# Normalizing attention weights inside the product that turns them, by a diagonal of reciprocal sums

## What is computed

```
# even layer of the first stack ("diff"): 4 heads, 2 components of width 64, values of width 128, causal, blocks of 128 queries
p = softmax(q k^T)                       # (component, query, key)
w = p[0] - lam * p[1]
out = w @ v
# odd layer ("odd"): 3 dilated patterns, 4 heads of width 128; a query sees up to 512 + 128 + 128 keys, one softmax over all of them
# second stack, even layer ("rope"): 8 query heads on 2 key heads of width 64, 256 context + 512 latent keys
sc = q k^T * scale;  pr = softmax(sc);  out = pr @ v
```

## Time and profile before

| | |
|---|---|
| median of 3 executions | 3251.61 us (3250.78 to 3253.14) |
| profiled execution: its time, its span | 3251.17 us, 3249.4 us |
| mean granted TensorE clock | 0.996 of full |
| TensorE busy (matmul, weight load) | 3195.2 us (98%), 2817.9 us (87%) |
| VectorE, ScalarE, GpSimd busy | 2307.3 us (71%), 1490.6 us (46%), 513.2 us (16%) |
| "diff", first score to the next slab | 182.87 to 230.28 us |
| "odd", two passes, first turn to the next slab | 751.34 to 779.85 us, 885.54 to 913.40 us |
| "rope", second scores to the next slab | 1932.64 to 2008.22 us |

### The profile page before, as it was taken

One profiled execution on the slowest core, in us unless ns is written; L12 is line 12 of the kernel. 1 busy time (PEld: TensorE's weight loads), 2 busy tenths in 40 slices (PEclk: granted clock), 3 DMA queues, 4 the chain that ended last, 5 costly groups with the idle time before them and its releaser, 6 DMA issues.

```text
span 3249.4 us, 52099 instructions
## 1 busy us (share of the span) xinstructions
PE 3195.2 (98%) x19134; PEld 2817.9 (87%) x19134; DVE 2307.3 (71%) x3350; ACT 1490.6 (46%) x2445; POOL 513.2 (16%) x363
## 2 busy tenths in 40 slices
PE   8989999999999999999999999999999999999999
PEld 6769888888888888898988987999999999899998
DVE  6567988764479976777777786768677667368665
ACT  5464433363554333544443466445344435444343
POOL 1111222110112221432100122210021001111000
PEclk9999999999999999999999999999999999999999
DMA  4203556521226553553334320222232223222232
GB/s 156 78 27 117 196 199 215 211 93 65 88 89 213 200 193 125 181 184 141 128 132 171 129 82 27 91 104 92 101 121 96 87 103 130 99 83 91 104 104 104
DMA packets 70385, 402.39 MB, mean 124 GB/s; under 512 B 7696, under 2 KB 10400, under 8 KB 31776
## 3 DMA queue, kind: packets, MB, share of 16 engines
q1 hardware_dynamic: 46544, 317.80, 27.6%
q10 hardware_dynamic: 23632, 81.73, 7.5%
HBM read 397.41 MB, written 2.10 MB: 123 GB/s over the span
## 4 chain that ended last, share of the span: by engine, by line
PE 93%; DVE 3%; issue 2%; DMA 1%; ACT 1%; DVEq 0%; SPq 0%; ACTq 0%
PE banks L704 13%; PE banks L706 13%; PE banks L705 13%; PE banks L613 7%; PE banks L820 7%; PE banks L822 6%; PE banks L821 6%; PE banks L614 6%; PE banks L615 6%; PE banks L702 2%; PE banks L745 1%; PE banks L747 1%; PE banks L746 1%; PE banks L701 1%; DMA mraw<-mod_stream 1%
## 5 line engine op out<-in xcount | busy, mean ns | idle before, releaser
L3112 POOL TENSOR_TENSOR wlo<-raw,whi 128x512 fp32r<-128x512 f32 (+1 forms) x217 | 318.7, 1469 | 2307.2 <-ACT whi L1312 1544.8
L704 PE MATMUL banks<-h_hi,whi 128*128 128x512 f32 x1376 | 543.1, 395 | 2.8 <-issue 1.3
L705 PE MATMUL banks<-h_lo,whi 128*128 128x512 f32 x1376 | 536.8, 390 | 0.0
L706 PE MATMUL banks<-h_hi,wlo 128*128 128x512 f32 x1376 | 536.7, 390 | 0.0
L1312 ACT ACTIVATE whi<-raw 128x1024 fp32r<-128x1024 f32 (+1 forms) x205 | 214.8, 1048 | 449.8 <-PE banks L706 218.3
L2083 DVE TENSOR_TENSOR wlo<-raw,whi 128x1024 fp32r<-128x1024 f32 (+1 forms) x217 | 309.4, 1426 | 17.9 <-ACT whi L1314 17.8
L2430 DVE SCALAR_TENSOR_TENSOR banks<-mraw,crow 128x1024 f32<-128x1024 f32 x188 | 268.5, 1428 | 72.8 <-DMA mraw<-mod_stream 58.0
L704 PEld LDWEIGHTS banks<-h_hi,whi 128*128 128x128 f32 x1376 | 258.7, 188 | 62.9 <-issue 8.8
L705 PEld LDWEIGHTS banks<-h_lo,whi 128*128 128x128 f32 x1376 | 258.9, 188 | 54.1 <-issue 1.9
L706 PEld LDWEIGHTS banks<-h_hi,wlo 128*128 128x128 f32 x1376 | 258.7, 188 | 54.1
L820 PE MATMUL banks<-xhi,whi 128*128 128x256 f32 x1024 | 291.7, 285 | 5.1 <-ACT crow L1620 5.1
(11 more groups left out here) (418 smaller groups left out, 7967.1 us busy)
## 6 DMA issues: line engine op xcount, KB each, us to landing
raw<-stream SPq DMA_DIRECT2D x297, 1024.0 KB, 4.8
mraw<-mod_stream ACTq DMA_DIRECT2D x144, 512.0 KB, 3.9
x<-xT SPq DMA_DIRECT2D x8, 256.0 KB, 6.8
out<-x SPq DMA_DIRECT2D x8, 256.0 KB, 2.0
ko<-k_odd ACTq DMA_DIRECT2D x1, 1152.0 KB, 5.3
raw<-stream SPq DMA_DIRECT2D x2, 512.0 KB, 5.7
crow<-c_rows ACTq DMA_DIRECT2D x1, 1024.0 KB, 4.8
cx<-ctxT SPq DMA_DIRECT2D x1, 1024.0 KB, 7.6
```

Of the source, the lines that this page charges most:

```text
L704: mm(o, hi, a_hi[:, kc, 0:T], start=(kc == 0), stop=False)
L705: mm(o, hi, a_lo[:, kc, 0:T], start=False, stop=False)
L706: last = mm(o, lo, a_hi[:, kc, 0:T], start=False, stop=(kc == K - 1))
L3112: G.tensor_tensor(wlo[:, slot, 0:wd], raw[:, slot, 0:wd], whi[:, slot, 0:wd].bitcast(F32), ALU.subtract)\
```

## The change

The scaled copies `dW`/`oW`/`aW` are gone. VectorE takes the reciprocals and multiplies the identity by them: a diagonal `dD`/`oD`/`aD` of 128 x 128, two of them in "diff" (the second with the factor minus lambda folded in by a second scalar). The turn is no longer a transpose but a plain matmul, with the unscaled probabilities as the stationary operand and the diagonal as the moving one; in "diff" two such products accumulate in PSUM. The exponentials now wait for the turn of an earlier unit instead of its weights, and in "odd" and "rope" the probabilities have three buffers.

```diff
 TensorE, diff and odd
-                        last = nc.tensor.transpose(aux[b // 4][:, (b % 4) * P:(b % 4) * P + P],
-                                                   w_ap[:, n % 2, b * P:(b + 1) * P], ident)
+                        for c in range(ncomp):
+                            last = mm(aux[b // 4][:, (b % 4) * P:(b % 4) * P + P],
+                                      p_ap[:, n % slots, c * S + b * P:c * S + b * P + P], diag[:, n % 2, c, :],
+                                      start=(c == 0), stop=(c == ncomp - 1))
 TensorE, rope
-                        last = nc.tensor.transpose(aux[k % 3][:, b * P:(b + 1) * P],
-                                                   aW[:, n % 2, (3 * half + b) * P:(3 * half + b + 1) * P], ident)
+                        last = mm(aux[k % 3][:, b * P:(b + 1) * P],
+                                  aP[:, n % 3, (3 * half + b) * P:(3 * half + b + 1) * P], aD[:, n % 2, :], start=True,
+                                  stop=True)
 ScalarE, diff and odd
-                    if n >= n0 + 2:
-                        act.wait_ge(sems["weights"], n - 1)
+                    slots = p_ap.shape[1]
+                    if n >= n0 + slots:
+                        act.wait_ge(sems["turned"], n - slots + 1)
 ScalarE, rope
-                if n >= 2:
-                    act.wait_ge(sem_a["weights"], n - 1)
+                if n >= 3:
+                    act.wait_ge(sem_a["turned"], 2 * n - 4)
 VectorE, diff
                         link(V.reciprocal(small[:, 44:46], sums))
-                        link(V.scalar_tensor_tensor(out=small[:, 46:47], in0=small[:, 45:46], scalar=small[:, 5:6],
-                                                    in1=ones[:, 0:1], op0=ALU.mult, op1=ALU.mult))
-                        link(V.tensor_scalar(w_ap[:, b, 0:w], p_ap[:, b, 0:w], small[:, 44:45], None, ALU.mult))
-                        V.scalar_tensor_tensor(out=w_ap[:, b, 0:w], in0=p_ap[:, b, S:S + w], scalar=small[:, 46:47],
-                                               in1=w_ap[:, b, 0:w], op0=ALU.mult, op1=ALU.add)\
+                        V.tensor_scalar(diag[:, b, 0, :], ident, small[:, 44:45], None, ALU.mult)
+                        V.tensor_scalar(diag[:, b, 1, :], ident, small[:, 45:46], small[:, 5:6], ALU.mult, ALU.mult)\
                             .then_inc(sems["weights"], 1)
 VectorE, odd
-                        V.tensor_scalar(w_ap[:, b, 0:w], p_ap[:, b, 0:w], small[:, 44:45], None, ALU.mult)\
+                        V.tensor_scalar(diag[:, b, 0, :], ident, small[:, 44:45], None, ALU.mult)\
                             .then_inc(sems["weights"], 1)
 VectorE, rope
-                V.tensor_scalar(aW[:, b, :], aP[:, b, :], small[:, 44:45], None, ALU.mult).then_inc(sem_a["weights"], 1)
+                V.tensor_scalar(aD[:, b, :], ident, small[:, 44:45], None, ALU.mult).then_inc(sem_a["weights"], 1)
```

More of the change, by code:

```diff
@@ L362, in build @@
         _, *dtmp = scope([("below", [P, 24 * S + S + 256 + NEVEN + 4 * S + 16 + 2 * S]),
-                          ("dP", [P, 2, 2 * S]), ("dW", [P, 2, S]), ("dWT", [P, 2, S])])
-        oq, okk, ov, ko, ko_r, oP, oW, oWT, oo = scope([
+                          ("dP", [P, 2, 2 * S]), ("dD", [P, 2, 2, P]), ("above_dD", [P, S]), ("dWT", [P, 2, S])])
+        dP, dD, _, dWT = dtmp
+        oq, okk, ov, ko, ko_r, oP, oD, _, oWT, oo = scope([
             ("oq", [P, 6, S]), ("okk", [P, 6, S]), ("ov", [P, 3, TT, 256]), ("ko", [P, NODD]), ("ko_r", [P, NODD], F32R),
-            ("oP", [P, 2, 768]), ("oW", [P, 2, 768]), ("oWT", [P, 2, 768]), ("oo", [P, 4, S])])
+            ("oP", [P, 3, 768]), ("oD", [P, 2, 1, P]), ("above_oD", [P, S]), ("oWT", [P, 2, 768]), ("oo", [P, 4, S])])
         near_qlo, _, near_klo, _, _, near_qhi, near_khi = scope([
@@ L369, in build @@
             ("below_near", [P, 6 * S]), ("near_qhi", [P, 2, S], F32R), ("near_khi", [P, 2, S], F32R)])
-        qa, kall, vall, pp, pa, pb, pd, _, ka, wpool, rot, aP, aW, aWT = scope([
+        qa, kall, vall, pp, pa, pb, pd, _, ka, wpool, rot, aP, aD, _, aWT = scope([
             ("qa", [P, 4, S]), ("kall", [P, CTX + S]), ("vall", [P, 6, P]), ("pp", [P, 4, 16 + S]),
             ("pa", [P, 16 + S]), ("pb", [P, 16 + S]), ("pd", [P, 4, S]), ("below_ka", [P, NROT]), ("ka", [P, NA - NROT]), ("wpool", [P, 4, P]),
-            ("rot", [P, 2, S]), ("aP", [P, 2, 768]), ("aW", [P, 2, 768]), ("aWT", [P, 4, 768])])
+            ("rot", [P, 2, S]), ("aP", [P, 3, 768]), ("aD", [P, 2, P]), ("above_aD", [P, S]), ("aWT", [P, 4, 768])])
         _, q_hi = scope([("below_q_hi", [P, PAD_MID + 38 * S + 24]), ("q_hi", [P, 4, S], F32R)])
@@ L905, in first_score, with attention @@
                 scores(n0, acc[(n0 + last_slab + 1) % 2]).then_inc(sems["scores"], 1)
-            def attention(sems, n0, end, scores, nblocks, w_ap, mix, name, last_slab):
+            def attention(sems, n0, end, scores, nblocks, p_ap, diag, mix, name, last_slab):
+                slots, ncomp = p_ap.shape[1], diag.shape[2]
                 def score(n):
@@ L1074, in diff_mix @@
                     last = mm(aux[2 + hd % 2][:, t * P:(t + 1) * P], bv[:, b, hd * P:(hd + 1) * P],
-                              dtmp[2][:, n % 2, b * P:(b + 1) * P], start=(b == 0), stop=(b == t))
+                              dWT[:, n % 2, b * P:(b + 1) * P], start=(b == 0), stop=(b == t))
                 return last
-            attention(sem_diff, 0, 16, diff_scores, lambda n: DIFF_U[n][1] + 1, dtmp[1], diff_mix,
+            attention(sem_diff, 0, 16, diff_scores, lambda n: DIFF_U[n][1] + 1, dP, dD, diff_mix,
                       "even_in", slab_of("even_in", 12))
@@ L1125, in _ @@
                 slab_tokens(s + 8, (s + 8) % 2, toks, after={1: odd_first})
-                attention(sem_odd, 8 * ps, 8 * ps + 8, odd_scores, lambda n: 6, oW, odd_mix,
+                attention(sem_odd, 8 * ps, 8 * ps + 8, odd_scores, lambda n: 6, oP, oD, odd_mix,
                           f"odd_in{ps}", slab_of(f"odd_in{ps}", 8))
@@ L1688, in expo @@
                         w = width(n)
-                        last = A(p_ap[:, b, c * S:c * S + w], scores[:, c * S:c * S + w], ACT.Exp,
+                        last = A(p_ap[:, n % slots, c * S:c * S + w], scores[:, c * S:c * S + w], ACT.Exp,
                                  bias=small[:, SM_MAX + 2 * b + c:SM_MAX + 2 * b + c + 1],
@@ L1818, in diff_after @@
                     split_hi(SPLIT["even"][0] + j, h_hi[:, j, :])
-            attention(sem_diff, 0, 16, lambda n: (DIFF_U[n][1] + 1) * P, 2, dtmp[0], dtmp[2], slab_of("even_in", 12), diff_after)
+            attention(sem_diff, 0, 16, lambda n: (DIFF_U[n][1] + 1) * P, 2, dP, dWT, slab_of("even_in", 12), diff_after)
             diff_out(3)
@@ L1961, in a_exp @@
                 act.wait_ge(sem_a["negmax"], n + 1)
-                if n >= 2:
-                    act.wait_ge(sem_a["weights"], n - 1)
+                if n >= 3:
+                    act.wait_ge(sem_a["turned"], 2 * n - 4)
                 b = n % 2
-                A(aP[:, b, :], flat[b][:, 0:768], ACT.Exp, bias=small[:, SM_MAX + b:SM_MAX + b + 1],
+                A(aP[:, n % 3, :], flat[b][:, 0:768], ACT.Exp, bias=small[:, SM_MAX + b:SM_MAX + b + 1],
                   accum_out=small[:, SM_SUM + 4 * b:SM_SUM + 4 * b + 1]).then_inc(sem_a["probs"], 1)
@@ L2562, in head_norm, with attention @@
                         head_out(name, i - 2, srcs[i - 2], gain, srcs[i - 2])
-            def attention(sems, n0, end, ncomp, p_ap, w_ap, nblocks, after, last_slab, only_first=False):
+            def attention(sems, n0, end, diag, nblocks, after, last_slab, only_first=False):
+                ncomp = diag.shape[2]
                 def negmax(n):
@@ L2580, in weights @@
                         dve.wait_ge(sems["turned"], n - 1)
-                    w = nblocks(n) * P
                     sums = small[:, SM_SUM + 4 * b:SM_SUM + 4 * b + ncomp]
@@ L2801, in _ @@
             dve.wait_ge(hn["out"], HN["gla"][0] + 4)
-            attention(sem_diff, 0, 16, 2, dtmp[0], dtmp[1], lambda n: DIFF_U[n][1] + 1, lambda n: None,
+            attention(sem_diff, 0, 16, dD, lambda n: DIFF_U[n][1] + 1, lambda n: None,
                       slab_of("even_in", 12))
@@ L2862, in _ @@
                 s = slab_of(nm, 8)
-                attention(sem_odd, 8 * ps, 8 * ps + 8, 1, oP, oW, lambda n: 6, None, s, only_first=True)
+                attention(sem_odd, 8 * ps, 8 * ps + 8, oD, lambda n: 6, None, s, only_first=True)
                 dve.wait_ge(slab_done, s + 1)
@@ L2882, in odd_after @@
                         odd_lo({9: 0, 10: 1, 14: 2}[n])
-                attention(sem_odd, 8 * ps, 8 * ps + 8, 1, oP, oW, lambda n: 6, odd_after,
+                attention(sem_odd, 8 * ps, 8 * ps + 8, oD, lambda n: 6, odd_after,
                           slab_of(nm, 8))
```

## The result

| | before | after |
|---|---|---|
| median, us | 3251.22 (3250.78 to 3253.14, 4 runs) | 3276.74 (3275.63 to 3277.60, 4 runs) |
| profiled span, us | 3249.4 | 3275.1 |
| granted clock, mean | 0.996 | 0.997 |

The changed kernel takes 1.0080 times as long, with a 95% interval of 1.0068 to 1.0092: some 25.5 us more. The forecast of slower, at 3279 in 3268 to 3289, holds.

The account below looks back on a forecast made before the run. TensorE was taken to bound the kernel (93% of the chain of waits), with something to win on VectorE in "diff" alone. "odd" 10.0, "rope" 17.2 and "diff" 0 sum to +27.2 us: 3279, range 3268 to 3289.

Parts of the forecast that it names:

- Price of a block: TensorE's turn of one block: 0.11 to 0.224 us in "odd" and "rope", to 0.448 in "diff"; two records a product.
- The first rival: A plain product keeps a transpose's pace, 0.11 us: about -10 us, 3242; chance 4%.
- the third: Rival: a plain product costs four transposes, 0.44 us: together +106 us, 3357; chance 3%.
- odd: Stage "odd": each six-block turn +0.68 us, fourteen charged in full, the first of each pass +0.25: sum +10.0 us.
- rope: Stage "rope": a step goes from 4.31 to 5.64 us, fourteen steps +15.7, with the ends +17.2 us.
- The other loop: In "rope", scores, negmaxes and exponentials: stays at 4.31 us a step and ends over a microsecond earlier.
- diff: Stage "diff": 44.8 us of TensorE work plus 3.0 idle, 47.8 us, +0.4; VectorE's saving is spent on TensorE.
- The tail: Half clock lasting from "diff" into the next slab, a loss of 1.0 us and some more; stage and tail together 0.
- The second rival: The half clock stays or spreads in "diff": +7 us and no better tail, 3286; chance 8%.
- Waits: Exponentials' new waits for an earlier unit's turn cost nothing; no transfer is moved.
- Sum: Whole kernel: 10.0 + 17.2 + 0 = 27.2 us, giving 3279.
- The fourth rival: Most added records hide behind unseen waits: below 0.2%, 6.5 us; chance 3%.

Follow-up runs that it names:

- e1: The kernel before, with each transpose written as a plain product with the identity and VectorE's scaling kept: 3277.66 us, ratio 1.0086.
- e6: The kernel before, with 36 unread products of the identity ahead of the waits for the weights in "diff": 3248.03 us, ratio 0.9995.
- e7: The kernel before, with 72 unread transposes of the identity ahead of the waits for the weights in "diff": 3247.04 us, ratio 0.9992.
- e2: The changed kernel, with turns by transposes of the unscaled first component, diagonals made but not used: 3240.11 us, ratio 0.9968.
- e4: The changed kernel, with probabilities and diagonals of the rounded type float32r in all three stages: 3247.59 us, ratio 0.9989.

## Why the prediction was right, step by step

- **Price of a block.** 0.224 us and two records a product: 762.04 to 763.38 for six. e1 shows that it is the whole loss. The first rival (the pace of a transpose) and the third (four times its price) fall with it. The Trainium skill's factor of four ("TensorE: Matmul & The Clock Gate", Terms) does not show here: 1.34 us for 0.66 is a factor of two.
- **odd.** Forecast +10.0, measured +9.8 (+4.8 and +5.1). The first turn is followed at once by the mask, with no wait for ScalarE: the 0.43 us of the earlier trace rows hid its part. I had credited nothing for shorter waits for VectorE, and named 9.3 if the first wait of each pass shrank by 0.33. That happened in one pass of the two: the wait of 0.66 us ahead of the second turn, in this row of the kernel before, is 0.32 after (at 757.88). e1, which keeps VectorE's work, has +10.2.
```profile
758.68 0.64 PEld L922 LDWEIGHTS banks<-kp,oW 128*128 128x128 f32 x6 [0.66 <-DVE oW L2595]
```
- **rope.** Forecast +17.2, measured +16.25. The step is 5.58 us, forecast 5.64. The turn takes 2.87 where I had 2.69 for the records, 0.08 for a plain load and 0.17 for a gap: what follows the last record's pace is 0.18 in all, so the 0.08 was counted twice. Fourteen times 0.06 is 0.8 of the 0.95 us of error; the steps at the two ends gave +0.2 and +1.2 for a forecast of +0.2 and +1.3. That the gap of 0.17 ahead of the scores stays without a wait was right. The other loop never bounds.
- **diff.** Forecast 47.8, measured 47.22: TensorE busy for 45.5 us where I had 44.8 of work, idle for 1.7 where I left 3.0, so two errors partly cancel. The clock is at 1.00. The tail's half clock went too. I had set stage and tail to 0 with up to +1 for a fall at the end; no fall came, and the two are worth -0.8 (-0.2, and -0.6 from 230.22 to 750.64). The second rival, the half clock stays, falls; e1, e6 and e7 show that it goes with idle time.
- **Waits.** ScalarE's new waits for the turn cost nothing that shows: e1, which has none of them, is as long in each stage to 0.4 us, and e2, which has them all, is 11 us faster than before in the stages.
- **Sum.** 27.2 forecast, 25.7 between the spans: 0.95 of the difference in "rope" and 0.8 in "diff" and its tail, 0.2 in "odd"; against these stand 0.45 more, outside the stages and the tail. The fourth rival, hidden records, falls by the loss itself: 25.5 us, not below 6.5.

## What to carry to other kernels

Ask which engine ends each stage before work is moved between engines: in "diff", "odd" and "rope" the same edit was worth -8.2, -0.4 and -2.6 us on VectorE's side (e2 less before) and +8.0, +10.2 and +18.8 on TensorE's (after less e2), the clock's part in "diff" included. A transpose that becomes an fp32 product doubles its records; if the scaling must go into the turn, round both operands first, if the lower precision of the attention weights can be borne. Where TensorE waits a microsecond or two for another engine, look at the clock behind the wait: a few unread products in it gave back 4 us of a stage of 47. Then look at the whole program: its median fell by only 1.3 us in e6 and 2.3 in e7, neither clear of no change.

## What the runs showed of the hardware that was not expected

- The clock's fall is part of a stage's price: 5 of 47 us in "diff" before. Each fall in the eleven traces had idle time of TensorE shortly ahead of it, but not each idle stretch is followed by one: from 1935 to 1937 TensorE was busy 0.64 us before and 0.57 in e4, the wait was 1.67 us before and 1.57 in e4, and only e4 fell. The kernel before in these windows, and its wait:
```profile
1935.00:1937.00 2.00, 0.64 (x4) 0.31 (x3) 1.77 (x4) 1.89 (x6) 1.90 (x2) 1.00 0.00 0
1937.00:1939.00 2.00, 1.93 (x18) 1.62 (x18) 1.83 (x3) 1.25 (x5) 1.98 (x2) 1.00 0.00 0
```
```profile
1937.07 0.19 PEld L1190 LDWEIGHTS banks<-k_hi,q_hi 64*128 64x128 f32 x2 [1.67 <-ACT aP L1965]
```
- A product of two float32r operands is one record at the same 0.11 us as a transpose (in e4's "odd", six from 768.03 to 768.70).
- An operation on VectorE of 0.29 us took 1.20 where GpSimd was at work on its own tiles, in the changed kernel as in the kernel before; these timeline rows of the changed kernel have such a one. The cause is inferred from their overlap and wasn't tested.
```profile
198.18 1.20 DVE L2595 TENSOR_SCALAR dD<-kp,small 128x128 f32<-128x128 f32 x1
```
```profile
198.03 1.27 POOL L3212 TENSOR_TENSOR stg<-gt,sag 128x512 f32<-128x512 f32 x1
```
